# Two attentions with bias and maximum in one operation, a scan with its steps in the tokens, on one core

## The reference, cut to what matters

```
# grouped attention, 4 query heads on 2 key heads, dim 64, no mask
o_a = softmax(rope(norm(q)) @ rope(norm(k)).T * 64**-0.5) @ v

# bidirectional scan, 4 heads of 64 channels, 2 groups of state 128; for each direction
acs    = cumsum(dt * a)                                   # dt > 0, a < 0
y[l]   = sum over s <= l of (C[l] . B[s]) * exp(acs[l] - acs[s]) * dt[s] * x[s]
y      = y_forward + y_backward + d_skip * x
o_b    = rms_norm(y * silu(z))

# differential attention, 4 heads, two maps of dim 32 each, a bias by relative position
p1 = softmax(q1 @ k1.T * 32**-0.5 + bias)
p2 = softmax(q2 @ k2.T * 32**-0.5 + bias)
o_c = rms_norm((p1 - lam * p2) @ v) * (1 - lam_init)
```

## Time and profile before

| what | us |
|---|---|
| median of 3 runs (4303.75 to 4304.28) | 4304.12 |
| the profiled execution's own time | 4301.26 |
| its span | 4299.5 |
| PE busy | 3726.2 (87%) |
| VectorE busy | 1848.1 (43%) |
| ScalarE busy | 1155.7 (27%) |

### The profile page before, as it was taken

The page is one execution under the profiler, slowest core; times in us unless marked ns, Lnnn a source line. Parts: engine busy times, 40 slices in busy tenths (PEclk is TensorE's granted clock), DMA queues, the critical chain, the costliest instruction groups (busy, mean ns, idle before and its releaser), DMA issues. The chain is left out here.

```text
span 4299.5 us, 45769 instructions
## 1 busy us (share of the span) xinstructions
PE 3726.2 (87%) x17216; PEld 2449.3 (57%) x17216; DVE 1848.1 (43%) x2894; ACT 1155.7 (27%) x1827; POOL 41.6 (1%) x20
## 2 busy tenths in 40 slices
PE   8899999798999897468986999989655997799997
PEld 6678778656787574136864343357313786533435
DVE  6465534584654444673333111153567333211115
ACT  6432222374222212343321000031234332100003
POOL 0000000120000000000000000000000000000000
PEclk9999999899999898678997999999776899799999
DMA  4223222102232220001214999922000222499991
GB/s 156 64 93 97 88 84 77 50 2 81 90 96 90 93 66 35 0 18 67 98 62 181 421 414 409 415 110 72 27 0 20 77 98 96 182 420 412 410 415 51
DMA packets 109582, 616.51 MB, mean 143 GB/s; under 512 B 12518, under 2 KB 13030, under 8 KB 59660
## 3 DMA queue, kind: packets, MB, share of 16 engines
q1 hardware_dynamic: 109452, 614.76, 37.7%
HBM read 610.76 MB, written 3.95 MB: 143 GB/s over the span
## 5 line engine op out<-in xcount | busy, mean ns | idle before, releaser
L385 PE MATMUL PS<-WK_r,RING_r 128*128 128x512 f32 x1824 | 715.9, 393 | 0.0
L383 PE MATMUL PS<-WK_r 128*128 128x512 f32 x1504 | 595.1, 396 | 76.5 <-DVE RING_r L380 76.5
L385 PEld LDWEIGHTS PS<-WK_r,RING_r 128*128 128x128 f32 x1824 | 346.0, 190 | 73.3
L383 PEld LDWEIGHTS PS<-WK_r 128*128 128x128 f32 x1504 | 286.4, 190 | 150.1 <-DVE RING_r L380 87.0
L380 DVE TENSOR_TENSOR RING_r<-RING,WK_r 128x1024 fp32r<-128x1024 f32 x214 | 261.5, 1222 | 218.6 <-ACT WK_r L377 218.6
L377 ACT ACTIVATE WK_r<-RING 128x1024 fp32r<-128x1024 f32 x214 | 225.4, 1053 | 464.5 <-PE PS L385 401.7
L2220 DVE TENSOR_TENSOR XT<-XT,PS 128x512 f32<-128x512 f32 x128 | 88.1, 688 | 579.1 <-PE PS L2146 579.1
L384 PE MATMUL PS<-HT_r,WK_r 128*128 128x512 f32 (+1 forms) x800 | 313.2, 392 | 0.0
L385 PE MATMUL PS<-AR_r,RING_r 128*128 128x512 f32 x672 | 263.4, 392 | 0.0
L383 PE MATMUL PS<-AR_r,RING_r 128*128 128x512 f32 x640 | 251.2, 393 | 10.3 <-DVE HT_r L380 10.3
L384 PE MATMUL PS<-AR_r,WK_r 128*128 (+1 forms) x592 | 234.1, 396 | 0.0
(11 more groups left out here) (393 smaller groups left out, 5718.7 us busy)
## 6 DMA issues: line engine op xcount, KB each, us to landing
AR<-moe SPq DMA_DIRECT2D x288, 1024.0 KB, 10.7
RING<-moe SPq DMA_DIRECT2D x96, 1024.0 KB, 11.3
RING<-ff_in SPq DMA_DIRECT2D x96, 512.0 KB, 3.6
RING<-branch SPq DMA_DIRECT2D x64, 640.0 KB, 3.9
RING<-ff_out SPq DMA_DIRECT2D x48, 512.0 KB, 3.6
RING<-mix_in SPq DMA_DIRECT2D x32, 512.0 KB, 3.6
RING<-ple SPq DMA_DIRECT2D x16, 640.0 KB, 12.7
RING<-nsa_in SPq DMA_DIRECT2D x16, 512.0 KB, 3.6
```

Source lines behind the costliest of these rows:

```text
L383: nc.tensor.matmul(out, r(w_high), r(x_high), start=start, stop=False)
L385: return nc.tensor.matmul(out, r(w_low), r(x_high), start=False, stop=stop)
```

## The change

In `att_*` the negated scores come straight from PSUM. With a bias, one `tensor_tensor_reduce` for each map adds the bias and takes the minimum; without one, the maximum is reduced straight from PSUM and the exponential reads PSUM, so that the copy is gone. The scale of the differential attention and its sign go into the eviction of the projections in `mix_project` (the operation becomes `scalar_tensor_tensor`), and the bias table is stored negated. Scores of item n wait for the exponentials of item n-2 in `grouped`.

In the scan the steps are multiplied into the channels (`XF` and `XB`, four operations in `ssm_prepare`), so the decays need no multiplication by them. Forward and backward parts stay apart in a buffer of five blocks of 128 columns (three such buffers), and `y` is two matmuls of together 640 columns. Two heads of one group take turns, so that the products are computed once for two heads. The mask is added for a whole head at once, the exponentials off the diagonal read PSUM, and the silu of `z` moves to `ssm_prepare`.

```diff
@@ mix_project, eviction of 16 units
-                    nc.vector.tensor_tensor(ar(n), bank(n % 4), R, ALU.mult).then_inc(s["free"], 1)
+                    scale = -DIFF_D ** -0.5 if n in (CQ, CQ + 1) else 1.0
+                    nc.vector.scalar_tensor_tensor(out=ar(n), in0=bank(n % 4), scalar=scale, in1=R,
+                                                   op0=ALU.mult, op1=ALU.mult).then_inc(s["free"], 1)
@@ att_pe, score
-            pe.wait_ge(s["maxed"], before + n + 1)
+            if n >= 2:
+                if items[n].bias is None:
+                    pe.wait_ge(s["exped"], 2 * (n - 1))
+                else:
+                    pe.wait_ge(s["maxed"], 2 * (n - 1))
@@ att_act, exps
+                if items[n].bias is None:
+                    ins = nc.scalar.activation(buf, bank(2 * (n % 2) + m), ACT.Exp, bias=NM[n % 3][:, m:m + 1],
+                                               accum_out=RS[n % 3][:, m:m + 1])
+                else:
+                    ins = nc.scalar.activation(buf, buf, ACT.Exp, bias=NM[n % 3][:, m:m + 1], scale=-1.0,
+                                               accum_out=RS[n % 3][:, m:m + 1])
@@ att_dve, shift
-            for ins in x.shift(SB[n % 3][:, :, 0:x.width], PS[:, 2 * (n % 2):2 * (n % 2) + 2, 0:x.width]):
-                step.count(ins)
-            step.wait()
-            nc.vector.tensor_reduce(NM[n % 3], SB[n % 3][:, :, 0:x.width], X, ALU.max, negate=True).then_inc(s["maxed"], 1)
+            if items[n].bias is None:
+                nc.vector.tensor_reduce(NM[n % 3], PS[:, 2 * (n % 2):2 * (n % 2) + 2], X, ALU.max, negate=True).then_inc(s["maxed"], 1)
+                return
+            if n >= 3:
+                dve.wait_ge(s["turned"], n - 2)
+            for m in range(2):
+                nc.vector.tensor_tensor_reduce(SB[n % 3][:, m], bank(2 * (n % 2) + m), items[n].bias, 1.0, 3e38,
+                                               ALU.add, ALU.min, NM[n % 3][:, m:m + 1]).then_inc(s["maxed"], 1)
@@ ssm_prepare
+                for c in range(2):
+                    nc.scalar.activation(ar(SZ + c), ar(SZ + c), ACT.Silu).then_inc(s["gate_z"], 1)
...
-                    v.tensor_copy(XK[:, :, c * P:(c + 1) * P],
-                                  bank(1 + c).rearrange("p (t c) -> p t c", t=TT)).then_inc(s["out_t"], 1)
+                    x = heads(bank(1 + c).rearrange("p (t c) -> p t c", t=TT))
+                    for d, out in enumerate((XF, XB)):
+                        dt = SCS[:, 2, :, 4 * d + 2 * c:4 * d + 2 * c + 2].unsqueeze(3).to_broadcast([P, TT, 2, 64])
+                        v.tensor_tensor(heads(out[:, :, c * P:(c + 1) * P]), x, dt, ALU.mult).then_inc(s["out_t"], 1)
@@ ssm_scan
+        ITEMS = [(g, sb, hh) for g in range(2) for sb in range(TT) for hh in range(2)]
+        EX = [WK[:, 4 * TOK + b * 5 * P:4 * TOK + (b + 1) * 5 * P] for b in range(3)]
+        MR = [[wk(8 + 2 * hh + d) for d in range(2)] for hh in range(2)]
+                rows(0)
+                rows(1)
+                products(0)
+                products(1)
+                for n, (g, sb, hh) in enumerate(ITEMS):
+                    if g == 0 and sb == TT - 1:
+                        pe.wait_ge(s["exped"], exps(n))
+                        rows(2 + hh)
+                    h = 2 * g + hh
+                    y = bank(6 + g)[64 * hh:64 * hh + 64]
+                    pe.wait_ge(s["weighted"], 2 * n + 2)
+                    nc.tensor.matmul(y[:, sb * P:], XF[:, sb, h * 64:(h + 1) * 64], EX[n % 3][:, (sb + 1) * P:],
+                                     start=(sb == 0), stop=(sb == TT - 1), skip_group_check=True)
+                    nc.tensor.matmul(y[:, 0:(sb + 1) * P], XB[:, sb, h * 64:(h + 1) * 64], EX[n % 3][:, 0:(sb + 1) * P],
+                                     start=False, stop=(sb == TT - 1), skip_group_check=True).then_inc(s["y_in"], 1)
+                    if hh and n // 2 + 2 < 2 * TT:
+                        products(n // 2 + 2)
...
+                    act.wait_ge(s["masked"], 2 * h + 2)
+                    if n >= 3:
+                        act.wait_ge(s["y_in"], n - 2)
+                    if sb:
+                        nc.scalar.activation(out[:, 0:sb * P], bank(2 * hh + 1, 0, sb * P), ACT.Exp, bias=bwd).then_inc(s["exped"], 1)
...
+                mask(0)
+                mask(1)
+                for n, (g, sb, hh) in enumerate(ITEMS):
+                    if g == 1 and sb == 0:
+                        mask(2 + hh)
+                    dve.wait_ge(s["exped"], exps(n))
+                    dve.wait_ge(s["g_in"], n // 2 + 1)
+                    b, f = EX[n % 3][:, 0:(sb + 1) * P], EX[n % 3][:, (sb + 1) * P:]
+                    v.tensor_tensor(f, f, G(n // 2)[:, sb * P:], ALU.mult).then_inc(s["weighted"], 1)
+                    v.tensor_tensor(b, b, G(n // 2)[:, 0:(sb + 1) * P], ALU.mult).then_inc(s["weighted"], 1)
+                    if n == 10:
+                        gated(0)
+                gated(1)
@@ the stage of the bias table
-                nc.vector.tensor_copy(wk(10, 7)[:, n * HALF:(n + 1) * HALF], bank(n % 7, 0, HALF)).then_inc(s["out_copied"], 1)
+                nc.vector.tensor_scalar(wk(10, 7)[:, n * HALF:(n + 1) * HALF], bank(n % 7, 0, HALF), -1.0, None, ALU.mult
+                                        ).then_inc(s["out_copied"], 1)
```

More of the change, by code:

```diff
@@ L958, in build, with __init__, att_pe @@
     class Item:
[L962 to L967, removed]
-        def score(n):
-            pe.wait_ge(s["maxed"], before + n + 1)
+        def __init__(self, scores, bias, weigh, values, outs):
+            self.scores, self.bias, self.weigh, self.values, self.outs = scores, bias, weigh, values, outs
+    def att_pe(pe, s, items):
+        maps = len(items[0].values)
+        def score(n):
+            if n >= 2:
[3 more added lines that the diff above has]
+                    pe.wait_ge(s["maxed"], 2 * (n - 1))
             for m, (q, k) in enumerate(items[n].scores):
-                mm = nc.tensor.matmul(bank(2 * (n % 2) + m, 0, items[n].width), q, k, start=True, stop=True)
+                mm = nc.tensor.matmul(bank(2 * (n % 2) + m), q, k, start=True, stop=True)
             mm.then_inc(s["scored"], 1)
         def turn(n):
[L975 to L978, removed]
+            pe.wait_ge(s["weighed"], maps * (n + 1))
+            if n:
+                pe.wait_ge(s["copied"], n)
             for m in range(maps):
-                for kb in range(len(x.values[m])):
-                    mm = nc.tensor.transpose(bank(6 + m, kb * P, P)[0:x.rows],
-                                             SB[n % 3][:, m, kb * P:kb * P + x.rows], cst("ident"))
+                for kb in range(TT):
+                    mm = nc.tensor.transpose(bank(6 + m, kb * P, P), SB[n % 3][:, m, kb * P:(kb + 1) * P], cst("ident"))
             mm.then_inc(s["turned"], 1)
@@ L986, in values @@
             x = items[n]
-            pe.wait_ge(s["copied"], before + n + 1 + COPIED)
-            blocks = len(x.values[0])
-            for kb in range(blocks):
+            pe.wait_ge(s["copied"], n + 1)
+            for kb in range(TT):
                 for m, out in enumerate(x.outs):
-                    mm = nc.tensor.matmul(out, x.values[m][kb], PT[n % 2][0:x.rows, m, kb * P:kb * P + P],
-                                          start=x.first and kb == 0, stop=x.final and kb == blocks - 1)
+                    mm = nc.tensor.matmul(out, x.values[m][kb], PT[n % 2][:, m, kb * P:kb * P + P],
+                                          start=(kb == 0), stop=(kb == TT - 1))
             mm.then_inc(s["summed_v"], 1)
@@ L1040, in att_dve @@
                 shift(n + 1)
-            dve.wait_ge(s["exped"], 2 * (before + n + 1))
+            dve.wait_ge(s["exped"], 2 * (n + 1))
             step(nc.vector.reciprocal(RC[n % 3], RS[n % 3]))
-            for ins in items[n].weigh(step, SB[n % 3][:, :, 0:items[n].width], RC[n % 3], CO[n % 3]):
+            for ins in items[n].weigh(step, SB[n % 3], RC[n % 3], CO[n % 3]):
                 ins.then_inc(s["weighed"], 1)
@@ L1604, in ssm_prepare @@
         AC = SM[0:8, 100:104]
-        with stage("padded copied_in conv silu act_step a_ready e_ready sums steps_t x_t out_t dve_step") as (block, s):
+        with stage("padded copied_in conv silu gate_z act_step a_ready e_ready sums steps_t x_t out_t dve_step") as (block, s):
             @block.scalar
@@ L1690, in _, with rows @@
+        EX = [WK[:, 4 * TOK + b * 5 * P:4 * TOK + (b + 1) * 5 * P] for b in range(3)]
+        MR = [[wk(8 + 2 * hh + d) for d in range(2)] for hh in range(2)]
+        exps = lambda n: sum(4 - (sb in (0, TT - 1)) for _, sb, _ in ITEMS[0:n + 1])
+        G = lambda q: bank(4 + q % 2)
+        with stage("rows_in masked g_in exped weighted y_in dve_step gated squared summed mean root inverse normed") as (block, s):
             @block.tensor
             def _(pe):
-                for h in range(SSM_H):
-                    if h >= 2:
```

(4 more changed lines are left out.)

176 lines of the change are left out of this document (59 added, 117 removed).

## The result

| kernel | median us | runs | span of the profiled run, us |
|---|---|---|---|
| before | 4304.20 (4303.75 to 4305.53) | 4 | 4299.5 |
| after | 4211.34 (4210.31 to 4214.78) | 4 | 4213.0 |

The account below looks back on a forecast made before the run. VectorE was taken to pace the attentions, with PE close behind in the grouped one and slowed by clock dips. Terms 3.4 + 16 + 19.6 - 1.3 = 37.7 us a layer, 75.4 in all, gave 4228 us (range 4205 to 4256).

Parts of the forecast that it names:

- Grouped, 3.4: Grouped attention: PE becomes the bound, giving back 0.20 us a period and waits at both ends; 3.4 us a layer gained.
- Preparation, +1.3: Scan's preparation: four multiplications out of PSUM replace two copies of together 1.28 us; 1.3 us a layer lost.
- Scan, 19.6: Scan: the last y ends 18.2 us earlier and the tail saves 1.4; 19.6 us a layer gained.
- 16 x 1.3: Scan: y's matmul pairs on PE, 16 items at 1.3 us each, every item priced alone.
- PE is the bound: Scan: PE's 36.8 us of work at full clock, 1.8 us and more an item, exceeds VectorE's and ScalarE's.
- Differential, 16: Differential attention: an item takes 2.87 us instead of 3.96, and the start gains 2 to 3; 16 us a layer gained.
- Eviction with a factor, negated table: 0: Projections' eviction in mix_project and bias table: no cost, at worst 1 us a layer and 0.5 once.
- (A): Rival for the three stages: PE's clock keeps dipping, gain only 27.6 us a layer, 4249 us; chance 0.15.
- over 0.9 after the first 15 us: Sign in grouped attention, scan and differential attention: granted clock over 0.9 after each stage's first 15 us.
- (B): Rival for the scan: each half of y costs a whole matmul's 1.0 us; 26.5 us a layer, 4251; chance 0.08.
- (C): Rival: PE never leaves its low level in the three stages; 40 us a layer slower, 4384 us; chance 0.02.
- (D): Rival for the scan: a missed wait in its new order leaves near no gain there; 4268 us; chance 0.05.

Follow-up runs that it names:

- a8: Changed kernel with both heads of a group writing y into the same column half (half the output not computed): 4218.59 us, ratio 0.9798.
- a5: Changed kernel with each of the scan's 8 products computed twice into the same bank: 4220.93 us, ratio 0.9798.
- b1: Changed kernel with two items' y matmuls in fours, both wide ones first, then both others, once both are weighed: 4221.25 us, ratio 0.9806.
- a3: Changed kernel, but in the differential attention PE waits for the bias table before its first scores: 4212.08 us, ratio 0.9784.
- a2: Only the scan and its preparation as in the changed kernel, everything else as before the change: 4258.29 us, ratio 0.9893.
- b2: Changed kernel plus unused matmuls on PE: ten ending the preparation, five in the scan's norm, four while the attention awaits the bias tables: 4206.41 us.
- b3: Changed kernel with the bias tables' transfer issued in the scan behind the second gate, not at the differential attention's start: 4203.49 us, ratio 0.9767.
- a4: Changed kernel with six idle 128x512 matmuls on PE at the end of the scan's preparation: 4210.33 us, ratio 0.9781.
- a6: Changed kernel with the scan's row matmuls over all 128 partitions (added rows zero) instead of 8: 4209.61 us, ratio 0.9774.
- b4: Changed kernel with rows over 128 partitions, bias tables fetched in the scan, and unused matmuls bridging PE's idle stretches: 4196.67 us, ratio 0.9746.

## Why the prediction was right, step by step

The direction held, the order of the parts did in layer 0, and so did the mechanism in the attentions; in the scan PE as the bound was only partly true. The sum was 17.5 us short, since two terms were under-sized.

- **Grouped, 3.4.** Measured 4.4 of 69.0 (69.0 to 64.7), from the periods (0.27 and not 0.20 each) and the last wait (0.27 for 1.26). The new wait at the start cost 1.18, as walked through.
- **Preparation, +1.3.** Measured +1.4: four operations of 0.69 start 0.6 apart. The multiplication out of PSUM costs the copy's time with the broadcast steps too.
- **Scan, 19.6.** Measured 25.2 and 19.6. The last `y` ended 38.3 us after the start where I had 43.9: the first `y` 1.0 sooner, and 4.6 less for the rest. The term that failed is "16 x 1.3" for `y`, 20.8. In layer 0's timeline the eight double items keep PE for 16.9 together: alone an item costs 1.15 to 1.25, and where the second is ready in time, two take 1.35, which the one half of a8 undoes. "PE is the bound" was only partly true once this was so (a5, b1). The tail lost 1.4, as forecast (from the last `y` to the tables' issue 11.2 before, 9.9 after). Layer 1's agreement with 19.6 is an accident: the fall of the clock took what the side-by-side work gave, and by this much luck the whole came nearer to the forecast.
- **Differential, 16.** Measured 21.9 and 20.0. The period was right: 2.86 for 2.87, with the pair at 1.22 for 1.23. What was missed is the start: about 4 us a layer from scores computed during the transfer (a3). The prediction's 2 to 3 us for the start stood for the earlier maximum alone. What is left beyond, 2 us in layer 0 and none in layer 1, I can't divide between the last item and the clock's rise.
- **Eviction with a factor, negated table: 0.** Measured 0 (151.4 and 151.4 for `mix_project` in layer 0).

**The rivals.** (A) "The clock keeps dipping" did not hold where it was put, at PE's short waits: with waits of 0.2 to 0.33 in every other item the clock stood at 1.00. But the clock does fall in the `y` phase in 12 of the 20 layers of the new scan with thin rows (over 8 partitions), always behind the second group's first rows and with PE busy. It stays down for 3.4 to 10.2 us; in a2, b2, b3, a4 and the changed kernel, where nothing else lengthens that phase, this costs 1.1 to 4.2 us. In the four layers with rows over 128 partitions (a6, b4) no such fall came; four are few. The sign "over 0.9 after the first 15 us" failed in layer 1's scan (0.82), while PE was busy for 97% of both `y` phases. So what I had named as the sign of my being wrong occurred, and not behind waits; in size it was a fifth of rival A's. (B) Splitting `y` does not pay: wrong, it costs less than I had taken. (C) and (D) did not occur; the new waits cost 1.18 once and 0.89 to 0.98 once a layer. The point from which (C) decides was worked out wrongly: 170 us against 105 is 62% of PE's work at the low level, and not 58%. By the Read-Write Bubble rule of the Trainium skill (Advanced Engine Details and Errata) the pair would have cost a latency more; the 1.22 us say no, as for the pair in the earlier trace rows.

## What to carry to other kernels

Price a matmul with 64 output columns as half an array: two that follow each other into different halves ran in nearly the time of one here (1.35 us for two items, 1.22 for one). But an order that only makes them meet can lose: b1 let every pair meet and was 9.9 us slower, since the loop through the buffers then set the pace. When a semaphore's source moves, look not only at the steady loop but at what the old one held back at the stage's start; here that was 4 us a layer, and the transfer behind it another 4. Once other waits are gone, see what kind of work PE does where its clock falls: being busy with thin matmuls did not always keep the clock up. And judge such a fall by several layers and runs, since it comes in some and not in others.

## What the runs showed of the hardware

- **Thin matmuls and the clock.** From idle, with rows over 8 partitions the granted clock was up 11.5 to 11.8 us after the scan's start and the first `y` came after 10.8 us (changed kernel, both layers); over 128 partitions it was up after 4.8 to 5.0 and the first `y` came after 8.0 to 8.1 (a6, both layers), with the same columns. From 1.00, behind a gap of 2.0 us, the rows over 8 partitions saw it fall to 0.50 for 6.8 us in both layers (b2); the full ones saw no fall in one layer, and behind a gap of 2.3 us one of 3.4 us in the other (b4). In the steady attention the thin scores (32 partitions) are 1.1 of 2.9 us, and the clock stays. Whether such scores alone let it fall is not shown: in b4 it fell in layer 0, 1.0 us after they began, and in layer 1 only in a wait. The Trainium skill's clock gate section (TensorE: Matmul & The Clock Gate, Part 1: The HAM clock gate) speaks of how busy PE has been recently. In b2 the clock fell with PE busy for 2.91 and then 3.00 of 3.00 us, so with a6 and b4 beside it, it depended on the rows used as well. What of a thin matmul the chip looks at is not settled by these runs, nor why the fall behind the second rows comes in some layers and not in others.
- **Side by side in the columns.** 1.35 us for two float32 items of 640 columns into different halves (changed kernel), 2.30 into the same one (a8).
- **Gaps.** In a gap of 5.4 us in PE the full clock was lost (a4); one of 2.0 us did not lose it by itself (b4, layer 0).
